# A table of slots for the recurrence parts, and both pairs' mixed products on ScalarE, in the scan of a hybrid layer

## The reference, cut to what matters

```python
def rwkv7_scan(inputs, s0):                      # 8 heads of 64, both directions
    def step(s, inp):
        r_t, w_t, k_t, v_t, kk_t, a_t = inp
        sa = jnp.einsum('bhvk,bhk->bhv', s, -kk_t)
        s = (s * w_t[:, :, None, :] + sa[..., None] * (kk_t * a_t)[:, :, None, :]
             + v_t[..., None] * k_t[:, :, None, :])
        return s, jnp.einsum('bhvk,bhk->bhv', s, r_t)

def rglru_direction(xb, lp, d, h0):              # 512 channels, both directions
    xc = causal_dwconv(xb.astype(jnp.float32), lp['conv_w'][d], lp['conv_b'][d])
    rg = jax.nn.sigmoid(block_diag_linear(xc, lp['wa'][d], lp['ba'][d]))
    ig = jax.nn.sigmoid(block_diag_linear(xc, lp['wx'][d], lp['bx'][d]))
    log_a = -LRU_C * rg * jax.nn.softplus(-lp['lam'][d])
    a = jnp.exp(log_a)
    bt = jnp.sqrt(-jnp.expm1(2.0 * log_a)) * (ig * xc)
    bt = bt.at[:, 0].add(a[:, 0] * h0)
    _, h = lax.associative_scan(lru_combine, (a, bt), axis=1)
```

## Time and profile before

| what | value |
|---|---|
| median of three runs | 3931.63 us (3924.51 to 3939.47) |
| profiled execution | 3922.09 us, of which span 3920.3 us |
| scan, first solve product to last keep | about 1128 to 2137 us of the span |
| TensorE, VectorE, ScalarE, GpSimd busy in the span | 3515.1, 2390.9, 1881.3, 1017.2 us |
| mean granted TensorE clock | 0.955 |
| copies to `FT`, ScalarE and VectorE | 90 each, 1.02 and 1.22 us |
| scan instructions L2933 | 72 |

### The profile page before, as it was taken

One profiled execution on the slowest core, in us unless ns is written; L12 is line 12 of the kernel. 1 busy time (PEld: TensorE's weight loads), 2 busy tenths in 40 slices (PEclk: granted clock), 3 DMA queues, 4 the chain that ended last, 5 costly groups with the idle time before them and its releaser, 6 DMA issues. The chain is left out here.

```text
span 3920.3 us, 93030 instructions
## 1 busy us (share of the span) xinstructions
PE 3515.1 (90%) x39677; PEld 3064.2 (78%) x39677; DVE 2390.9 (61%) x4313; ACT 1881.3 (48%) x3153; POOL 1017.2 (26%) x1042
## 2 busy tenths in 40 slices
PE   5699999999969889898896787993999999999997
PEld 2578888888858778777785787772899999999987
DVE  3236666560017888888887654335666667667676
ACT  3336566551116766667676443331444344434454
POOL 1313333331114444444421453001110101101102
PEclk8799999999979999999998898996999999999999
DMA  5235555552264555555553574333566766666786
GB/s 180 62 113 178 181 171 179 171 171 87 75 144 112 126 129 137 131 122 126 128 115 107 179 228 146 129 129 109 157 213 197 222 203 208 209 204 203 253 272 223
DMA packets 711777, 630.46 MB, mean 161 GB/s; under 512 B 198786, under 2 KB 620484, under 8 KB 710340
## 3 DMA queue, kind: packets, MB, share of 16 engines
q1 hardware_dynamic: 662212, 512.98, 44.4%
q0 software_dynamic: 22688, 80.75, 6.9%
q10 hardware_dynamic: 26464, 30.77, 2.6%
HBM read 462.75 MB, written 161.50 MB: 159 GB/s over the span
## 5 line engine op out<-in xcount | busy, mean ns | idle before, releaser
L431 DVE TENSOR_TENSOR moe_w_lo<-moe_w_lo_whole,moe_w_hi 128x2048 fp32r<-128x2048 f32 x254 | 446.5, 1758 | 241.6 <-ACT moe_w_hi L647 194.7
L579 PE MATMUL moe_h<-moe_xt_hi,moe_w_hi 128*128 128x256 f32 x2048 | 582.4, 284 | 6.9 <-DVEq L58 3.4
L579 PE MATMUL moe_h<-moe_xt_hi,moe_w_lo 128*128 128x256 f32 x2048 | 580.1, 283 | 0.0
L579 PE MATMUL moe_h<-moe_xt_lo,moe_w_hi 128*128 128x256 f32 x2048 | 580.1, 283 | 0.0
L1966 PE MATMUL inward_pp<-u_u_hi,inward_w_hi 128*128 128x512 f32 (+1 forms) x1360 | 527.0, 387 | 20.0 <-POOL inward_w_lo L2127 20.0
L1966 PE MATMUL inward_pp<-u_u_lo,inward_w_hi 128*128 128x512 f32 (+1 forms) x1360 | 515.5, 379 | 0.0
L1966 PE MATMUL inward_pp<-u_u_hi,inward_w_lo 128*128 128x512 f32 (+1 forms) x1360 | 515.1, 379 | 0.0
L579 PEld LDWEIGHTS moe_h<-moe_xt_hi,moe_w_hi 128*128 128x128 f32 x2048 | 393.2, 192 | 17.9 <-issue 5.9
L579 PEld LDWEIGHTS moe_h<-moe_xt_lo,moe_w_hi 128*128 128x128 f32 x2048 | 393.3, 192 | 3.6
L579 PEld LDWEIGHTS moe_h<-moe_xt_hi,moe_w_lo 128*128 128x128 f32 x2048 | 393.2, 192 | 0.0
L1966 PEld LDWEIGHTS inward_pp<-u_u_hi,inward_w_hi 128*128 128x128 f32 x1360 | 256.8, 189 | 79.3 <-POOL inward_w_lo L2127 20.3
(11 more groups left out here) (387 smaller groups left out, 8496.8 us busy)
## 6 DMA issues: line engine op xcount, KB each, us to landing
moe_w_lo_whole<-in_moe_w SPq DMA_DIRECT2D x384, 512.0 KB, 5.5
scan_by_parity<-scratch_ops SPq DMA_DIRECT2D x144, 192.0 KB, 4.3
scan_over<-scratch_ops SPq DMA_DIRECT2D x72, 384.0 KB, 4.2
inward_w_lo_whole<-in_w_in SPq DMA_DIRECT2D x38, 512.0 KB, 4.6
scratch_ops<-inward_ops_bk SPq DMA_DIRECT2D x72, 256.0 KB, 2.6
scratch_ops<-inward_ops_aq SPq DMA_DIRECT2D x72, 256.0 KB, 2.7
scan_aq<-scratch_ops SPq DMA_DIRECT2D x72, 256.0 KB, 2.8
scratch_gates<-inward_out SPq DMA_DIRECT2D x64, 256.0 KB, 2.2
```

What stands on the lines that cost most here:

```text
L431: return nc.vector.tensor_tensor(x_lo, x, x_hi.bitcast(F32), ALU.subtract)
L579: mm = nc.tensor.matmul(hb[ft % 2][m][:, 0:CAP], w_, x_, start=(k == 0 and part == 0), stop=(k == KD - 1 and part == 2))
```

## The change

Four things, all in `scan`:
1. VectorE's `forward` is removed; ScalarE's `forward` runs for both pairs, one after the other, at every level.
2. VectorE's recurrence parts come from a table over the slots of a pass, `RECURRENCE_AT`. Against before: series(k0) of chunk 0's piece moves from begin2 to the end of begin3, behind taps and gated input; keep moves one piece back and one slot where it stood with X or Z (begin2 has keep alone, F3 series alone, W3 keep ahead of the taps); recur is one piece later (k-5).
3. ScalarE: gates of chunk 0 move from start to begin0, directly ahead of squares; the window of W4 moves behind the copies of level 5; roots move from begin0 to behind that window, and take the pieces 4c-1 to 4c+2, in one operation.
4. The ring has eight slots, numbered from one piece earlier, so that the four pieces of a root never wrap.

```diff
+RECURRENCE_AT = {"start": ("series", "keep"), "begin0": ("taps",), "begin1": ("recur",), "begin2": ("keep",), "begin3": ("taps", "series"), "F1": ("recur",),
+                 "W1": ("series", "keep"), "F2": ("taps",), "W2": ("recur",), "F3": ("series",), "W3": ("keep", "taps"), "W4": ("recur",)}
...
-        RING, LAST_PIECE = 6, 2 * NG * NJ - 1
+        RING, LAST_PIECE = 8, 2 * NG * NJ - 1
...
+        def slot(k):
+            return (k + 1) % RING
...
-                (AC, DV)[u][u].wait(pe, f"F{m}", it)
+                AC[u].wait(pe, f"F{m}", it)
...
-            def forward(m, a):
-                u = 0
+            def forward(u, m, a):
                 PE[u].wait(act, f"T{m - 1}", a[0])
                 AC[u].did(f"F{m}", act.activation(FT[u][:, :, :], pair[u][:, :, :], ACT.Copy))
...
-            def roots(it):
-                DVq.wait(act, "q3", 4 * it + 3)
-                first = 4 * it % RING
-                for a, e in ([(first, first + 4)] if first + 4 <= RING else [(first, RING), (0, first + 4 - RING)]):
-                    act.activation(root[:, a:e, :], root[:, a:e, :], ACT.Sqrt).then_inc(s_root, 1)
+            def roots(group):
+                last = min(4 * group + 2, LAST_PIECE)
+                at, end = slot(max(4 * group - 1, 0)), slot(last) + 1
+                DVq.wait(act, "q3", last)
+                act.activation(root[:, at:end, :], root[:, at:end, :], ACT.Sqrt).then_inc(s_root, 1)
...
-                    if step == "X":
+                    if at == "begin0" or step == "X" and at != "start":
                         gates(k)
-                    elif step == "Z":
-                        if chunk == 0 and c[0]:
-                            roots(c[0] - 1)
+                    if step == "Z":
                         squares(k)
+                    elif step == "S":
+                        if at != "W4":
+                            window(k + 2)
...
                 for m in LEVELS:
                     if a is not None:
-                        forward(m, a)
+                        for u in U:
+                            forward(u, m, a)
+                    if c is not None and m == 5:
+                        window(4 * c[0] + 5)
+                        roots(c[0])
...
-            def forward(m, a):
-                u = 1
-                PE[u].wait(dve, f"T{m - 1}", a[0])
-                DV[u].did(f"F{m}", dve.tensor_copy(FT[u][:, :, :], pair[u][:, :, :]))
...
-                    if step == "X":
-                        if k:
+                    for part in RECURRENCE_AT[at]:
+                        if part == "series" and k:
                             series(k - 1)
-                        if k > 4:
-                            keep(k - 5)
-                    elif step == "Z":
-                        taps(k + 1)
-                        gated_input(k)
-                    elif c[0]:
-                        recur(k - 4)
+                        elif part == "keep" and k > 5:
+                            keep(k - 6)
+                        elif part == "taps":
+                            taps(k + 1)
+                            gated_input(k)
+                        elif part == "recur" and k > 4:
+                            recur(k - 5)
...
             series(LAST_PIECE)
-            keep(4 * LAST - 1)
-            for k in range(4 * LAST, 4 * LAST + 4):
+            keep(LAST_PIECE - 5)
+            for k in range(LAST_PIECE - 4, LAST_PIECE + 1):
                 recur(k)
                 keep(k)
```

More of the change, by code:

```diff
@@ L2346, in scan @@
         PE = [Steps(n.sem(f"pe_solve{u}"), ["L", "V"] + [f"{p}{d}" for p in FIRST_OF[u] for d in U] + ["tB", "tK"] + level_pe) for u in U]
-        AC = [Steps(n.sem(f"act_solve{u}"), ["L", "V", "tB"] + ([] if u else [f"F{m}" for m in LEVELS])) for u in U]
-        DV = [Steps(n.sem(f"dve_solve{u}"), [f"{x}{d}" for p in FIRST_OF[u] for d in U for x in EVICTED[p]] + ["tK"] + [x for m in LEVELS for x in ([f"F{m}", f"W{m}"] if u else [f"W{m}"])]) for u in U]
+        AC = steps("act_solve", ["L", "V", "tB"] + [f"F{m}" for m in LEVELS])
+        DV = [Steps(n.sem(f"dve_solve{u}"), [f"{x}{d}" for p in FIRST_OF[u] for d in U for x in EVICTED[p]] + ["tK"] + [f"W{m}" for m in LEVELS]) for u in U]
         PO = steps("pool_solve", ["W0"])
@@ L2763, in gates @@
                     DVs.wait(act, "scan", k - RING)
-                ACg.did("i", act.activation(gated[:, k % RING, :], bank[1][0][:, G:2 * G], ACT.Tanh, scale=0.5, bias=lru_col(5, j, d)))
+                ACg.did("i", act.activation(gated[:, slot(k), :], bank[1][0][:, G:2 * G], ACT.Tanh, scale=0.5, bias=lru_col(5, j, d)))
                 if k % NG == NG - 1 and k < LAST_PIECE:
@@ L2774, in squares @@
                     DVq.wait(act, "q3", k - 1)
-                ACq.did("decay", act.activation(decay[:, k % RING, :], th[:, :], ACT.Exp, scale=lru_col(0, j, d), bias=lru_col(0, j, d)))
+                ACq.did("decay", act.activation(decay[:, slot(k), :], th[:, :], ACT.Exp, scale=lru_col(0, j, d), bias=lru_col(0, j, d)))
                 ACq.wait(act, "decay", k)
-                ACq.did("sq", act.activation(sq[:, :], decay[:, k % RING, :], ACT.Square))
+                ACq.did("sq", act.activation(sq[:, :], decay[:, slot(k), :], ACT.Square))
                 ACq.did("la", act.activation(la[:, :], th[:, :], ACT.Identity, scale=lru_col(1, j, d), bias=lru_col(1, j, d)))
-                ACq.did("root", act.activation(root[:, k % RING, :], th[:, :], ACT.Identity, scale=lru_col(2, j, d), bias=lru_col(3, j, d)))
-            def roots(it):
-                DVq.wait(act, "q3", 4 * it + 3)
-                first = 4 * it % RING
-                for a, e in ([(first, first + 4)] if first + 4 <= RING else [(first, RING), (0, first + 4 - RING)]):
-                    act.activation(root[:, a:e, :], root[:, a:e, :], ACT.Sqrt).then_inc(s_root, 1)
+                ACq.did("root", act.activation(root[:, slot(k), :], th[:, :], ACT.Identity, scale=lru_col(2, j, d), bias=lru_col(3, j, d)))
+            def roots(group):
[3 more added lines that the diff above has]
+                act.activation(root[:, at:end, :], root[:, at:end, :], ACT.Sqrt).then_inc(s_root, 1)
             def store_z(j):
@@ L2797, in states @@
                     k = 4 * c[0] + chunk
-                    if step == "X":
+                    if at == "begin0" or step == "X" and at != "start":
                         gates(k)
-                    elif step == "Z":
-                        if chunk == 0 and c[0]:
-                            roots(c[0] - 1)
+                    if step == "Z":
                         squares(k)
+                    elif step == "S":
+                        if at != "W4":
+                            window(k + 2)
                         for j in range(NJ - 1):
-                            if k - 4 == 2 * NG * (j + 1):
+                            if k - 5 == 2 * NG * (j + 1):
                                 store_z(j)
-                    else:
-                        window(k + 2)
             def body(a, c):
@@ L2836, in _ @@
             through(act, body)
-            roots(LAST)
+            roots(LAST + 1)
             store_z(NJ - 1)
@@ L2907, in gated_input @@
             def gated_input(k):
-                x = gated[:, k % RING, :]
+                x = gated[:, slot(k), :]
                 ACg.wait(dve, "i", k)
@@ L2912, in series @@
             def series(k):
-                x = root[:, k % RING, :]
+                x = root[:, slot(k), :]
                 ACq.wait(dve, "root", k)
@@ L2923, in recur @@
                 j, d, m, i = lru_of(k)
-                x, before = root[:, k % RING, :], root[:, (k - 1) % RING, :]
-                dve.wait_ge(s_root, sum(1 + (4 * it % RING > 2) for it in range(k // 4 + 1)))
-                DVs.did("in", dve.scalar_tensor_tensor(out=x, in0=gated[:, k % RING, :], scalar=0.5, in1=x, op0=ALU.mult, op1=ALU.mult))
+                x, before = root[:, slot(k), :], root[:, slot(k - 1), :]
+                dve.wait_ge(s_root, (k + 1) // 4 + 1)
+                DVs.did("in", dve.scalar_tensor_tensor(out=x, in0=gated[:, slot(k), :], scalar=0.5, in1=x, op0=ALU.mult, op1=ALU.mult))
                 DVs.wait(dve, "in", k)
@@ L2932, in recur @@
                     start = before[:, G - 1:G] if d == 0 else before[:, 0:1]
-                DVs.did("scan", dve.tensor_tensor_scan(x[:, way], decay[:, k % RING, way], x[:, way], start, ALU.mult, ALU.add))
+                DVs.did("scan", dve.tensor_tensor_scan(x[:, way], decay[:, slot(k), way], x[:, way], start, ALU.mult, ALU.add))
             def keep(k):
@@ L2941, in keep @@
                 piece = z.rearrange("p (r w) -> p w r", w=GRID_W)[:, 8 * i:8 * i + 8, :]
-                h = root[:, k % RING, :].rearrange("p (w r) -> p w r", r=GRID_H)
+                h = root[:, slot(k), :].rearrange("p (w r) -> p w r", r=GRID_H)
                 if d == 0:
@@ L2975, in body @@
                         taps(0)
```

(2 more changed lines are left out.)

## The result

| | median of the runs | profiled execution |
|---|---|---|
| before | 3930.5 us (3924.5 to 3939.5) | 3922.1 us |
| changed | 3974.1 us (3971.0 to 3977.2) | 3971.0 us |

The ratio of the changed kernel to the one before is 1.0102, 95% interval 1.0076 to 1.0128: slower by 1.0%, 40 us by the ratio and 43.6 between the medians. The forecast was 3950, that is +18, with 3900 to 3978 as its range.

A forecast was written before the change was run, and what follows sets the result against it. A relay of three in-order engines was taken as the bound. Per pass +2.5 − 1.5 = +1.0 us, sixteen passes +16, the ends +2: +18 on the 3931.6 us median gives 3950, range 3900 to 3978.

The forecast's parts named there:

- the heavier rival: Same as "ScalarE becomes the bound": the sixteen passes lose 2.7 us each, 3977 us in all, chance 0.17.
- the signs named beforehand: If right: level-1 wait of 2 us or more, decay idle until E + 22, tK and merge waits gone, pass 54.6.
- Part 1: Roots behind level 5, whose products end at E: K 0.5 us late, masks from E + 8.5, chunk 1's X wait gone.
- Part 2: Series behind the taps on VectorE: level 1 begins 1.1 us earlier, but the series ends only at E + 22.1.
- my bound (1.2 for the slow series): At level 1, VectorE's whole chain with a slowed series: 1.2 us more, a loss of 3.7 a pass at most.
- Part 3: Level 1, second copy on ScalarE: TensorE waits 2.0 and 0.45 us for the copies; 2.5 us a pass lost up to there.
- The gains behind: Levels 2 to 5, after the level-1 loss: shorter waits win back 1.5 us a pass, between 0.8 and 2.5.
- Part 4: Ends of the scan: longer last pass and tail, first pass 1 us shorter, perhaps 1 from TensorE's clock; sum +2 us.
- ScalarE becomes the bound: Sixteen passes: slow series costs 1.2 us more and K waiting a full microsecond 0.5 more; +2.7 a pass, 3977, chance 0.17.
- It moves nothing: All passes: TensorE's waits only shift, 5.7 us before and 6.0 after; within 0.3 a pass, 3937 us, chance 0.14.
- the first rival: Same as "The gains win": 3910 us, chance 0.24; it counts 4.1 us a pass more for ScalarE.
- The gains win: Level 1 costs nothing if the series ends before E + 21.1; 1.5 us a pass gained, 3910 or 3892, chance 0.24.

The follow-up runs named there:

- series_before_taps: The changed kernel with the two entries of begin3 exchanged, so VectorE runs the series ahead of the taps; ratio 0.9998 to the kernel before, median 3924.1 us.
- squares_behind_copies: The changed kernel with ScalarE's squares of chunk 1's piece moved from begin3 to slot F1, behind both level-1 copies; ratio 1.0015 to the kernel before.

## Why the prediction was right, point by point

**How near it was.** 3974 lies 4 us inside the range, and that it lies there is partly luck. It is outside the forecast's own band (3935 to 3964), the loss is more than twice the +18 that was forecast, and the range reached so far up only because it took in the heavier rival, which did not come as described.

**Direction and cause: right.** "Behind them in ScalarE's queue stand both level-1 copies" is what the trace of the changed kernel shows, and `series_before_taps` and `squares_behind_copies` take it away from either side, the one by an earlier series and the other by another queue order. Of the signs named beforehand the level-1 wait, the idle decay (until E + 22.9), the places of the table loads and the vanished merge came; the wait for `tK` did not vanish (0.6 a pass at level 1), and the pass is 55.9, not 54.6.

**Part 1.** `r` was to end at E + 7.7 and the masks to begin at E + 8.5; they did at E + 7.2 and E + 7.9 (1412.48 + 0.47, and 1413.70 on VectorE). The second copy of level 5 ended where it should, but X and L went closer together. So K was 0.24 late instead of 0.5, and X of chunk 1 0.77 early where I had it as early as the old time less 0.3. The load for Tanh went where I put it, behind V's copies, and its 1.28 us are followed by the gate 0.01 later. The Trainium skill's drain ("ScalarE: Activation LUTs", "What ACT_TABLE_LOAD costs"), 1.38 us, does not appear here either; with it behind both loads K would, by an estimate from that figure, have been 3.0 us late instead of 0.24.

**Part 2.** Level 1's early start was forecast as 1.1 and measured as 1.16; the series' end as E + 22.1 and measured as E + 22.8. The 0.7 are the series itself: 1.92 from its first product's start to its end instead of 1.24, while GpSimd was busy for 7.09 of 8 us in that window. The rest cancels nearly: the copies of `tK` began 0.2 later than forecast, behind a keep of 1.59 instead of 0.7, and taps and gated input took 2.2 instead of 2.4 (the taps 1.95 instead of 1.61, the gated input 0.41 instead of 0.95). The Trainium skill ("GPSIMD Engine Reference", "Key points") says that GpSimd and VectorE contend for SBUF when VectorE reads two inputs from there; these operations do. The trace agrees with it: over the sixteen passes the first two operations of a series took 0.60 us in the median with a GpSimd operation beside them and 0.42 without. But no run here took GpSimd's work away. It was in my bound (1.2 for the slow series), not in my sum.

**Part 3, the step that was mis-sized.** "X of chunk 2 can't start before E + 27.6 ... Loss up to here: 2.5 us." Its start came 2.9 later than before by the medians of the table (2.3 by the means of sixteen passes), and there my list ended. But the level-1 products, X and the products behind it then ran at the lower clock: level 2 began 3.86 later (3.1 by the means). From the level-1 square products to Z of chunk 2 the changed kernel took 8.0 us in the mean, 5.3 of them at 1.2 GHz; `series_before_taps`, at the full clock there, took 6.6. So the lower clock cost some 1.4 us a pass in this stretch, an estimate from these two traces, and about as much is missing between forecast and measurement: the pass is +2.3 instead of +1.0, and sixteen of them +37 instead of +16. The gains behind were forecast as 1.5 and measured as 1.6 (3.86 to 2.23), though differently spread: 1.1 between levels 3 and 4 (forecast 0.45), 0.7 at level 5 (0.8), next to nothing at level 2. The clock behind the new wait is the term that I had put at nothing; I had weighed TensorE's clock only where the last body would gain from it.

**Part 4.** The last body with the tail was +2.8 to +3.8 in my list; with the seventeenth pass (2.3) taken off the 7.4, it is 5.1. The first pass was 2.3 shorter (57.8 against 60.2), forecast as 1. Together +2.8 against the +2 of the list, from one execution of each kernel.

**The rivals.** "ScalarE becomes the bound", 3977, gave the time best, but not by the mechanism it names: K waited 0.17, not a microsecond, and the series was 0.7 slower, not 1.2; the clock, which that rival does not name, makes up most of the rest. "It moves nothing" had the waits nearly right, 5.7 before and 6.0 after where 5.5 were measured; that list gives a pass +0.3, while the sum by slots gives +1.0, and the prediction left the two side by side. (It also has 5.1 us a pass for ScalarE in part 3 and 4.1 in the first rival; 4.3 was measured.) "The gains win" had its turning point at a series that ends before E + 21.1. `series_before_taps` ends it at E + 20.6 (1411.33, with E at 1390.73) and still waits 0.8 at level 1 and 0.7 before X of chunk 2. It came out at no difference, 0.9998. In the profiled executions its passes are 1.0 shorter than before; of those 16 us, 3 went again in the last pass and body and 4 behind the scan, and its execution lies 11 us below its median where the one of before lies 4 to 8 below.

## What to carry to other kernels

In a relay of in-order engines, ask of every moved operation who waits for its result and what stands behind the waiter in its own queue; here what the second question hides cost 1% of the time, and an exchange of two entries took it back. A sum of waits isn't their price on TensorE: two waits of 0.9 and 1.3 us a pass were cheaper than one of 2.0, behind which the granted clock fell in 10 of 16 passes, and in the changed kernel TensorE was idle no longer than before and yet lost 2.3 us a pass, for the most part by running slower. When a change has several parts, time them alone: the copy to ScalarE, by its busy times the plainest gain of the four, was worth nothing in the old order or in the right new one.

## What the runs showed of the hardware

TensorE's granted clock went to 1.2 GHz in each of the sixteen passes during or just behind a wait of 2.8 us (mean) in otherwise dense work, and stayed there for 3.4 or 6.8 us at a time; before, with waits of up to 2.0 us, it fell five times in sixteen passes. It is not the wait's length alone, nor the sum of the idle time: `squares_behind_copies` has no slot with a mean wait above 1.5 us and is idle for 3.8 us a pass, less than the 5.7 of the kernel before, and still stands at that level for 4.1 us a pass. Six of its nine falls came 31 to 33 us into the pass, behind the wait of 1.5 at level 2, and three at 46 to 50. Why the clock fell there stays unexplained.

In the scan's passes a table load of 1.28 us was followed by its operation 0.01 to 0.02 us later; in the last body of the kernel before the root started 0.55 us after its load had ended.
